# A two-layer decoder with routed experts: the order of expert weight loads around the first gather, and the place of six VectorE subtractions

## The reference

```python
for i in range(DEPTH):
    mix = swa_sink_attention(...) if i % N_MIXERS == 0 else forgetting_attention(...)
    x = layer_norm(ALPHA * x + mix, ln_gain[i, 0], ln_bias[i, 0])
    ffn = grouped_moe(x, w_router, b_router, w_gate[i], w_up[i], w_down[i])
    x = layer_norm(ALPHA * x + ffn, ln_gain[i, 1], ln_bias[i, 1])

# grouped_moe, for 512 tokens, 16 experts, 256 hidden columns each
hg = jnp.einsum('td,edf->tef', h2, w_gate)
hu = jnp.einsum('td,edf->tef', h2, w_up)
act = jax.nn.silu(hg) * hu * gate_dense[:, :, None]
y = jnp.einsum('tef,efd->td', act, w_down)
```

## Time and profile before

| | us |
|---|---|
| median of 3 runs | 919.23 (918.41 to 920.52) |
| the profiled execution's own time | 919.96 |
| its span | 918.2 |
| PE busy | 888.0 (97%) |
| DVE busy | 552.9 (60%) |
| ACT busy | 392.3 (43%) |
| POOL busy | 120.1 (13%) |

### The profile page before, as it was taken

The page is one execution under the profiler, slowest core; times in us unless marked ns, Lnnn a source line. Parts: engine busy times, 40 slices in busy tenths (PEclk is TensorE's granted clock), DMA queues, the critical chain, the costliest instruction groups (busy, mean ns, idle before and its releaser), DMA issues.

```text
span 918.2 us, 12501 instructions
## 1 busy us (share of the span) xinstructions
PE 888.0 (97%) x4480; PEld 616.2 (67%) x4480; DVE 552.9 (60%) x1141; ACT 392.3 (43%) x787; POOL 120.1 (13%) x138
## 2 busy tenths in 40 slices
PE   8999999999999999989999999999999999999996
PEld 7887777884666665557878886655786565666553
DVE  4544786548766677773332223777456777677846
ACT  4322787001555655540132224777301355555540
POOL 2000232103010000120000000323111200000030
PEclk9999999999999999999999999999999999999999
DMA  9962000019999998644054222120106999999352
GB/s 347 302 253 92 2 1 1 24 47 351 350 382 389 379 389 322 222 180 163 21 184 138 92 93 92 46 71 24 69 24 241 312 380 382 374 384 406 124 197 96
DMA packets 49446, 182.36 MB, mean 199 GB/s; under 512 B 6496, under 2 KB 6496, under 8 KB 41200
## 3 DMA queue, kind: packets, MB, share of 16 engines
q1 hardware_dynamic: 35712, 132.34, 38.6%
q0 software_dynamic: 9392, 34.12, 11.3%
q10 hardware_dynamic: 4288, 15.21, 4.2%
HBM read 159.60 MB, written 22.05 MB: 198 GB/s over the span
## 4 chain that ended last, share of the span: by engine, by line
PE 89%; DVE 5%; DMA 3%; issue 2%; ACT 1%; SPq 1%; POOL 0%; DVEq 0%; ACTq 0%; POOLq 0%
PE bank L613 17%; PE bank L615 16%; PE bank L614 16%; PE bank L896 11%; PE bank L727 4%; PE bank L708 4%; PE bank L865 3%; PE bank L570 3%; PE bank L752 2%; PE bank L771 2%; PE bank L527 2%; DMA ring<-in_swa_w_in 2%; PE bank L813 2%; PE bank L541 1%; DMA ys<-arena 1%
## 5 line engine op out<-in xcount | busy, mean ns | idle before, releaser
L1492 DVE TENSOR_TENSOR gu_low<-ring,gu_high 128x1024 fp32r<-128x1024 f32 x128 | 151.2, 1221 | 46.9 <-ACT gu_high L1116 46.8
L1116 ACT CAST gu_high<-ring 128x1024 fp32r<-128x1024 f32 x128 | 127.6, 1048 | 18.5 <-DVE arena L1626 18.5
L896 PE MATMUL bank<-ring,arena 128*96 128x512 f32 x256 | 115.8, 595 | 2.0 <-issue 2.0
L613 PE MATMUL bank<-gu_high,rows_high 128*96 128x512 f32 x256 | 113.0, 442 | 2.5 <-DVE rows_low L1610 2.5
L614 PE MATMUL bank<-gu_low,rows_high 128*96 128x512 f32 x256 | 101.5, 397 | 0.0
L615 PE MATMUL bank<-gu_high,rows_low 128*96 128x512 f32 x256 | 101.1, 395 | 0.0
L896 PEld LDWEIGHTS bank<-ring,arena 128*96 128x96 f32 x256 | 39.7, 164 | 55.0 <-issue 54.0
L1048 ACT ACTIVATE arena<-arena,nmax 128x256 f32<-128x256 f32 (+3 forms) x128 | 66.8, 523 | 20.9 <-DVE nmax L1385 10.8
L471 POOL TENSOR_TENSOR low<-ring,high 128x512 fp32r<-128x512 f32 x32 | 40.7, 1272 | 220.5 <-ACT high L1076 220.5
L613 PE MATMUL bank<-high,x_high 128*128 128x512 f32 x160 | 64.2, 401 | 1.3 <-DVE low L1286 1.1
L615 PE MATMUL bank<-high,xlow 128*128 128x512 f32 x160 | 62.9, 393 | 0.0
(11 more groups left out here) (244 smaller groups left out, 1543.7 us busy)
## 6 DMA issues: line engine op xcount, KB each, us to landing
ring<-in_w_gate SPq DMA_DIRECT2D x32, 1024.0 KB, 12.3
ring<-in_w_up SPq DMA_DIRECT2D x32, 1024.0 KB, 15.0
ring<-in_w_down SPq DMA_DIRECT2D x32, 1024.0 KB, 14.9
ring<-in_fox_w_in SPq DMA_DIRECT2D x6, 2048.0 KB, 9.4
ys<-arena ACTq DMA_DIRECT2D x28, 384.0 KB, 7.7
ys<-lnp POOLq DMA_DIRECT2D x1, 4608.0 KB, 24.3
ring<-in_swa_w_in SPq DMA_DIRECT2D x2, 2048.0 KB, 17.2
ring<-in_swa_w_o SPq DMA_DIRECT2D x2, 2048.0 KB, 15.9
```

Of the source, the lines that this page charges most:

```text
L613: eng.matmul(out, ah, wh, start=(c == 0), stop=False)
L896: mm = eng.matmul(bank[5 + half][0:CAP, :], hT[:, b, c, :], w[:, c, half * BLK:(half + 1) * BLK], start=(c == 0), stop=(c == FC - 1))
L1116: eng.copy(gu_high[u % 2][:, :, part, :], slot_gate_up(use)[:, :, part, :]).then_inc(S("gu_high"), 1)
L1492: eng.tensor_tensor(gu_low[use % RING][:, :, part, :], slot_gate_up(use)[:, :, part, :], gu_high[u % 2][:, :, part, :], ALU.subtract).then ...
```

## The change

It has two parts.

**Weight loads.** In both layers SP issues the down weights of expert 0 after `wo_done`, as before. All that came behind is held until the rows of expert 0 have been gathered (`xe_in{l}0`), and is put in another order: gate and up of 2, down of 1, gate and up of 3, down of 2. The down weights of expert 3 wait for the rows of expert 1.

**Splits.** DVE makes two of the eight low parts of the second value block where it made all eight, and the other six after the first tile's low rows are there (`state_low(0)`).

```diff
                 eng.wait_ge(S(f"wo_done{l}"), OUT_BLOCKS * NT)
-                for u in range(RING):
+                load_down(EXP_USE[l], l, 0, S(f"d_loaded{EXP_USE[l] % RING}"))
+                for u in range(1, RING):
+                    if u < RING - 1:
+                        eng.wait_ge(S(f"xe_in{l}0"), 16)
+                    else:
+                        eng.wait_ge(S(f"xe_in{l}1"), 16)
+                    if u + 1 < RING:
+                        k = EXP_USE[l] + u + 1
+                        load_gate_up(k, l, u + 1, S(f"w_loaded{k % RING}"))
                     k = EXP_USE[l] + u
-                    if u == RING - 1:
-                        eng.wait_ge(S(f"xe_in{l}1"), 16)
-                    if u >= OUT_BLOCKS:
-                        load_gate_up(k, l, u, S(f"w_loaded{k % RING}"))
                     load_down(k, l, u, S(f"d_loaded{k % RING}"))
...
                 if l + 1 < DEPTH:
-                    value_weights_low(KC, 2 * KC)
+                    value_weights_low(KC, KC + 2)
...
                             if b == 0 and t >= 1:
                                 state_low(t - 1)
+                                if t == 1:
+                                    value_weights_low(KC + 2, 2 * KC)
```

## The result

| | before | after |
|---|---|---|
| median, us | 918.82 (918.28 to 920.52, 4 runs) | 930.72 (929.96 to 933.41, 4 runs) |
| span of the profiled execution | 918.2 | 928.8 |
| PE busy | 888.0 | 890.9 |
| waits of PE in the down matmuls for DVE's copy | none in the view of waits | 9.5 |

The changed kernel takes 1.0127 times as long, with a 95% interval of 1.0103 to 1.0150. It is **slower by 11.9 us**. The prediction had the sign right but said 922.4, and the time lies above its range, which ended at 925.8.

What follows compares the result with a forecast made beforehand. PE, busy 97%, bounds the kernel, with DMA engines full through the experts. Gather -0.96, splits -1.6, late expert 4 loads +2.7 and +3.1 make +3.2 us: median 919.23 becomes 922.4, range 916.5 to 925.8.

Steps and rivals of the forecast that it cites:

- The view of what bounds the kernel: Whole kernel: PE busy 97% of the span; DMA engines have nothing to spare through the experts, so missed work isn't caught up.
- The gather, 0.96 us: First gather of each layer: may land earlier without weight loads, saving PE's 0.43 and 0.53 us idle, 0.96 at most.
- The splits, 1.6 us: End of layer 0: moving six subtractions removes PE's whole gap ahead of the first turned tile, 1.6 us.
- Up of 2 lands at 227.1 + 10.5 = 237.6 ... so that this load is just in time: Layer 0, expert 2: the held up load lands at 237.6, wanted by ACT's casts at 237.8.
- Expert 4 late by 2.9 us: Both layers: expert 4's up load lands 2.9 us late; PE loses 2.7 us in layer 0, 3.1 in layer 1.
- as good as full from 228 on: Upper bound on the loads' shift: the earlier start saves nothing, shift 13.6 us, each layer loses 5.3.
- The loads stay ahead: Rival, experts' loads: DMA engines make up for the empty stretch, only gains left, -2.6 us, 916.7, faster; chance 0.16.
- half as late: Rival, experts' loads: loss of 1 to 1.5 us per layer eats the gains, 919 to 920.5, no change; chance 0.20.
- The clock falls in the new gaps: Rival, PE's 2.7 us gap per layer: granted clock falls, up to 3.4 us more, 925.8, slower; chance 0.12.
- The gather isn't faster: Rival, first gather: the 0.96 us stays away and loads start 0.5 later, 923.9, slower; chance 0.06.

Runs made afterwards that it cites:

- released-by-row-numbers kernel: Changed kernel, but the held loads wait for DVE's row numbers, not the first gather's landing; 930.81 us, ratio 1.0109 to the kernel before.
- second kernel above: Kernel before with only the hold of the weight loads, subtractions as before; 933.15 us, ratio 1.0162.
- the one with filled gaps: Changed kernel plus 22 matmuls that nobody reads behind the turning of expert 2's rows; 929.01 us, ratio 1.0097 to the kernel before.
- the gathers spread out: Changed kernel, but POOL issues the gathers of experts 2 and 3 only when earlier rows are turned; 935.19 us, ratio 1.0164 to the kernel before.

## Why the prediction was right or wrong

**The view of what bounds the kernel: right.** That the DMA engines have nothing to spare through the experts decided the case. Any PE wait showed in full: gaps of 9.5 us and 2.8 of clock more than before, less 1.8 for the splits, are 10.5 of the 10.6 us of the span.

**The gather, 0.96 us: wrong, it is next to nothing.** With hardly anything else moving, the first gather takes the same 4.4 us, and PE's weight loads wait as before, 0.46 us in layer 0 (0.43) and 0.34 in layer 1 (0.53):

```profile
227.44 0.96 PEld L869 LDWEIGHTS bank<-ident,arena 96*128 96x128 f32 x8 [0.46 <-DMA arena<-xd,row_ids]
```

I had named the other end, "nothing if the 4.4 us are all latency", and it is that. The released-by-row-numbers kernel shows the other side: a crowd would cost 4.9 us, but in the kernel before there was none.

**The splits, 1.6 us: right**, with 1.8 in the traces and nothing late behind them. Tile 1's cover held.

**"Up of 2 lands at 227.1 + 10.5 = 237.6 ... so that this load is just in time": this is the step that failed.** It came at 242.6 and 739.2. The 10.5 us were read from loads that started at 230.06 in the kernel before. The queues' rows tell what the engines did from there until up of 3 landed, 10.4 us (230.06 to 240.5), and in the changed kernel from the release until up of 2 landed, 15.2 us (227.42 to 242.6):

```profile
q1 hardware_dynamic: 379, 2.47, 65.4%
q0 software_dynamic: 273, 0.98, 34.8%
```

```profile
q1 hardware_dynamic: 431, 2.68, 60.2%
q0 software_dynamic: 503, 1.74, 41.1%
```

The gathers had 0.348 x 10.44 = 3.6 us of the engines before and have 0.411 x 15.18 = 6.2 us now: 0.76 MB more of them, since the loads start 2.6 us earlier among gathers that had then not yet landed, **2.6 us**. The loads had 0.654 x 10.44 = 6.8 us and have 0.602 x 15.18 = 9.1 us, **2.3 us** more. Some 0.6 of these are for 0.21 MB more that moved, and 1.7 for the rate, 362 GB/s within their share before and 293 now. Together the two are the 4.7, but for the rounding of shares that add up to a little over 1. That the loads are slower while so many gathers run is seen in the second kernel above too (2.67 MB in 0.630 x 15.2 us, 279 GB/s); why, the traces don't tell. The gathers suffered as well: that of 226.74 took 9.5 us, its counterpart before 6.3. The remaining 0.3 of the 5.0 us by which the load missed its 237.6 are the release, at 227.42 and not at 227.1. I had seen the low rate of 259 GB/s at a share of 1.00 and used it for a bound on expert 4, but not for the load that came first. And "just in time" should have been a warning: a margin of 0.2 us at expert 2, on a term whose bounds were 3 us away, was passed over for the one at expert 4.

**Expert 4 late by 2.9 us: not in this kernel.** The stall of 4.7 us at expert 2 gave the engines that time back, so that the shift found its margin again: its up load lands at 237.15 + 26.4 = 263.6, where the casts of 264.50 could have begun at 263.8. The shift was mis-sized too, by the same low rate: it is 263.6 - 249.95 = 13.6 us where the sum took 10.7, and in layer 1 it is 733.75 + 26.1 - 742.6 - 4.2 (by which that layer starts later) = 13.0 where it took 11.3. The first is the prediction's own upper bound, "as good as full from 228 on", and the second is near it. By these numbers it was only the stall ahead of the load that kept it from costing PE. In the three profiles with gate and up of 2 not held the mechanism shows once, 3.4 us in one layer, and in the one with filled gaps once, 1.8 us in one layer. So it is a real cost, but one of other kernels than this.

**The rivals.** *The loads stay ahead* and *half as late*: no. *The clock falls in the new gaps*: the mechanism is right, in both layers, at 1.7 and 2.8 us, where I had allowed 1.7 in each, though the gaps stand at expert 2 and not at expert 4. I gave it 0.12, because a gap of 1.2 us had let the clock alone once and not the other time; the gaps of 4.6 us and more did it in each of the four profiles that have them, and one of 3.3 us with the gathers spread out did not (264 to 272 us, 1.00). *The gather isn't faster*: right, too.

**The range.** The text held the numbers for its upper end: 5.3 us per layer if "the engines were as good as full from 228 on", and up to 3.4 for the clock. Together, without other change, they give 919.23 - 0.96 - 1.6 + 10.6 + 3.4 = 930.7. That this meets the measured 930.72 is luck, since the gaps came at another expert and were 9.5, the gather gave nothing, and the clock added 2.8; but the size was within what the text had weighed. The range took the clock on top of the middle value and left the bound itself out, so that it ended at 925.8. Both hang on one cause, the gap of PE, so that they could come true together.

## What to carry to other kernels

Before you hold a load back from a stretch in which the DMA engines are idle, look at the load that is wanted first after it, and price it at the rate of the stretch into which it moves, with the gathers that are in flight there, not at the rate of the same loads elsewhere. A gather that already lands in its idle latency has nothing to win from a clear road. To a new wait of PE belongs what the clock costs behind it, and where two costs have one cause, the range has to hold both at once.

## What the runs showed that I had not expected

- The indirect gather of 96 rows of 4 KB takes 4.4 us from issue to landing with the engines as good as idle, no less than behind the last weight load in the kernel before, and 9.3 us with five loads of 1024 KB issued around it.
- At a DMA share of 1.00 to 1.04 the engines moved anything between 247 GB/s (228 to 232 of the changed kernel) and 419 (244 to 248): a share of 1 doesn't say what they move. Within their own share of the engines' time, loads of 1024 KB moved 293 GB/s among the gathers of five experts and 362 among fewer.
- The granted clock fell in some executions of one kernel and not in others at places with short gaps (150 to 160, 220 to 235, 720 to 735). The mean clock goes with most of the scatter of the kernel before (a correlation of -0.86 to -0.92).
- Filling PE's gap with matmuls kept its clock up in that gap, but paid less than the clock had cost. With the splits alone there was no gain. In the held kernel the profile gained 2.6 of 4.5 us, and the rest went mostly into one late load.
- Not each wait that a profile puts down to a load is a cost. Where an engine is idle for something else just as long, as ACT is for DVE's copy at every expert, only the time beyond that counts.

The fastest version is the splits alone, 0.1 to 0.3% under the kernel before in three groups of runs (0.9978, 0.9974 with the added matmuls, and 0.9988, whose interval reaches 1.0001).
